# Where the modulation sums of a two-block network stand: three feed-forward stages or two

## The reference, cut to what matters

```
sc, scc = silu(c), silu(c_ctx)
for layer in range(2):
    mod_l = (sc  @ ada_w[layer] + ada_b[layer]).reshape(-1, 9, 1024)
    mod_c = (scc @ ada_w[layer] + ada_b[layer]).reshape(9, 1024)
    x = half_ffn(x, mod[0], mod[1], mod[2], ...)      # x + 0.5*gate*swiglu(rmsnorm(x)*(1+scale)+shift)
    x = x + mod[5] * mixer(rmsnorm(x)*(1+mod[4]) + mod[3])
    x = half_ffn(x, mod[6], mod[7], mod[8], ...)
```

## Time and profile before

| | us |
|---|---|
| median of three runs (lowest, highest) | 2487.13 (2485.32, 2487.84) |
| the profiled execution | 2486.22 |
| its span | 2484.4 |
| TensorE busy | 2417.2 |
| VectorE busy | 1796.4 |
| stage 1, `up0`/`down0` | about 50 to 396 |
| stage 2, `up1`/`down1` | about 609 to 974 |
| stage 3, `up2`/`down2` | about 976 to 1340 |

### The profile page before, as it was taken

How to read it: one execution, slowest core, us unless ns; L and a number is a source line. 1 busy time by engine, 2 the same in 40 slices (tenths; PEclk the granted TensorE clock), 3 DMA queues, 4 the chain that set the end, 5 groups by cost and what they waited for, 6 DMA issues and landing times.

```text
span 2484.4 us, 36330 instructions
## 1 busy us (share of the span) xinstructions
PE 2417.2 (97%) x13814; PEld 2072.6 (83%) x13814; DVE 1796.4 (72%) x2889; ACT 598.9 (24%) x1163; POOL 5.0 (0%) x12
## 2 busy tenths in 40 slices
PE   7999999999999999999999999999998999999998
PEld 5888888767888888888888688888898999898887
DVE  5888887345777667886666568887787776788876
ACT  4000001162111001101002434412265513325401
POOL 0000000000000000000000000000000000000000
PEclk9999999999999999999999999999999999999999
DMA  7555555201444443555553226564543312455563
GB/s 277 173 165 177 173 175 199 90 1 51 152 146 141 143 149 97 183 166 175 168 180 122 90 68 187 187 195 152 157 128 94 103 60 87 135 169 186 183 196 109
DMA packets 98478, 359.65 MB, mean 145 GB/s; under 512 B 10880, under 2 KB 12160, under 8 KB 96832
## 3 DMA queue, kind: packets, MB, share of 16 engines
q1 hardware_dynamic: 96480, 350.37, 45.0%
q0 software_dynamic: 848, 6.77, 0.7%
q10 hardware_dynamic: 1040, 1.05, 0.1%
HBM read 357.10 MB, written 1.05 MB: 144 GB/s over the span
## 4 chain that ended last, share of the span: by engine, by line
PE 93%; DVE 4%; ACT 1%; issue 1%; DMA 0%; SPq 0%; DVEq 0%; ACTq 0%
PE lin L2119 20%; PE lin L2121 19%; PE lin L2120 19%; PE lin L2131 9%; PE lin L2132 5%; PE pair L2322 2%; PE lin L2349 1%; PE lin L2135 1%; PE lin L2205 1%; PE lin L2201 1%; PE lin L2202 1%; PE pair L2736 1%; PE pair L2723 1%; PE lin L2141 1%; PE lin L2143 1%
## 5 line engine op out<-in xcount | busy, mean ns | idle before, releaser
L2119 PE MATMUL lin<-h_all,whi 128*128 128x512 f32 (+1 forms) x1904 | 666.0, 350 | 11.1 <-DVE wlo L1501 5.9
L1501 DVE TENSOR_TENSOR wlo<-raw_all,whi 128x1024 fp32r<-128x1024 f32 (+1 forms) x525 | 631.0, 1202 | 43.0 <-ACT whi L1261 16.4
L2120 PE MATMUL lin<-h_all,whi 128*128 128x512 f32 (+1 forms) x1904 | 658.5, 346 | 0.0
L2121 PE MATMUL lin<-h_all,wlo 128*128 128x512 f32 (+1 forms) x1904 | 658.4, 346 | 0.0
L2119 PEld LDWEIGHTS lin<-h_all,whi 128*128 128x128 f32 x1904 | 361.6, 190 | 60.9 <-issue 9.2
L2120 PEld LDWEIGHTS lin<-h_all,whi 128*128 128x128 f32 x1904 | 361.8, 190 | 43.6
L2121 PEld LDWEIGHTS lin<-h_all,wlo 128*128 128x128 f32 x1904 | 361.4, 190 | 43.7
L1500 DVE CAST whi<-raw_all 128x1024 fp32r<-128x1024 f32 (+2 forms) x396 | 267.0, 674 | 152.0 <-PE lin L2121 109.0
L1890 DVE CUSTOM_DVE_ANT_0 std_all<-raw_all,cond_rows 128x1024 f32<-128x1024 f32 x224 | 273.5, 1221 | 3.3
L2119 PE MATMUL lin<-a_all,whi 128*128 128x512 f32 (+1 forms) x716 | 261.5, 365 | 4.2 <-DVE a_all L935 2.0
L2120 PE MATMUL lin<-a_all,whi 128*128 128x512 f32 (+1 forms) x716 | 260.2, 363 | 0.0
(11 more groups left out here) (374 smaller groups left out, 3030.4 us busy)
## 6 DMA issues: line engine op xcount, KB each, us to landing
raw_all<-w_up SPq DMA_DIRECT2D x176, 512.0 KB, 4.2
raw_all<-w_mod SPq DMA_DIRECT2D x128, 512.0 KB, 3.7
raw_all<-w_down SPq DMA_DIRECT2D x64, 512.0 KB, 4.0
raw_all<-w_exp_up SPq DMA_DIRECT2D x64, 512.0 KB, 3.8
raw_all<-w_exp_down SPq DMA_DIRECT2D x32, 512.0 KB, 4.2
raw_all<-w_down SPq DMA_DIRECT2D x32, 384.0 KB, 3.6
raw_all<-w_b_qk SPq DMA_DIRECT2D x24, 512.0 KB, 3.7
raw_all<-w_b_conv SPq DMA_DIRECT2D x24, 512.0 KB, 3.6
```

What stands on the lines that cost most here:

```text
L1501: dve.tensor_tensor(wlo[s][:, 0:n], r[:, 0:n], whi[s][:, 0:n].bitcast(F32), ALU.subtract)\
L2119: pe.matmul(out_, a, hi[n], start=start and n == 0, stop=False)
L2120: pe.matmul(out_, a, lo[n], start=False, stop=False)
L2121: ins = pe.matmul(out_, b, hi[n], start=False, stop=stop and n == len(cols) - 1)
```

## The change

The stages with tiles are now two, with 64 tiles each; stage 3 has none. So in stages 1 and 2 nearly every step from 4 to 66 has one tile (step 4 has two). Stage 3 loads its weights into all four slots, and its `up` part is a loop on VectorE and SyncE.

```diff
-REGIONS = (("up0", "down0"), ("up1", "down1"), ("up2", "down2"))
-REGION_GROUPS = ((1, 2, 3), (4, 5), (6, 7, 8))
+REGIONS = (("up0", "down0"), ("up1", "down1"))
+REGION_GROUPS = ((1, 2, 3, 4), (5, 6, 7, 8))
...
-                if ph in ("ffn0", "ffn1", "ffn2"):
+                if ph in ("ffn0", "ffn1"):
                     load_region(sp, int(ph[3]))
                     continue
```

## The result

| | median of the runs, us (lowest, highest) | profiled execution | its span |
|---|---|---|---|
| before | 2487.74 (2485.32, 2489.33), five runs beside those of after | 2486.22 | 2484.4 |
| after | 2500.17 (2498.20, 2501.65) | 2501.01 | 2498.8 |

The ratio is 1.0051, with a 95% interval of 1.0037 to 1.0065: 12.4 us slower. Forecast were 8.4 us, 2495.5 in a range up to 2499.0. So the sign was right and the time fell outside the range.

What follows compares the result with a forecast made beforehand. TensorE, busy 2417.2 of 2484.4 us, was taken as the bound. 4.87 + 1.27 + 1.4 + 0.9 = 8.4 us on the profiled 2486.22 gave 2494.7, as a median 2495.5 us; range 2490.3 to 2499.

Steps and rivals of the forecast that it cites:

- Inside stages 1 to 3: Within the three stages, moved sums cost or gain 0 us: TensorE fills the windows and VectorE's work still fits.
- The list of 14.83 us: VectorE's work for three `down0` steps: 14.31 us plus 0.52 for bias additions, fitting under TensorE's 14.96 us.
- The end of stage 1: `ab_uqk` 0 held behind the last tile load; VectorE stands 5.0 us, the last addition before the norm is 4.87 us late.
- The end of stage 2: Same queue order with one-vector tiles: `up2`'s first unit is late, the last addition before the norm 1.27 us late.
- The landing time: At the stage ends, a load behind a tile load lands 4.6 us after issue, as measured; the skill page's estimate was 4.0.
- the first term: Lateness of the last addition at the end of stage 1: 4.87 us, or 4.3 by the skill page's landing.
- TensorE's clock in these norms: Norms after stages 1 and 2: standstill lowers the clock, costing 1.4 us (2.3 if L2173 stays slow) and 0.9 us.
- A: Stage ends: late load mostly covered, landing in 3.7 us; 2491.4 us, or 2487.1 if the queue holds nothing; chance 0.12.
- B: Inside stage 1: VectorE becomes the bound, at 0.2 us over per pair adding 4.4 us, 2500 us; chance 0.06.
- C: Stage 3: matmuls speed up when 64 sums leave, a pair in 10.5 us instead of 10.88, 2482 us; chance 0.03.
- The 0.83 for slower: Whole kernel: chance 0.83 of slower by over 0.2%, against 0.14 within 0.2% and 0.03 faster.

Runs made afterwards that it cites:

- the emptied stage 3: The kernel before without stage 3's 48 tiles, that stage in four slots and loops, stages 1 and 2 keeping 48 and 32 tiles: 2487.67 us, ratio 1.0.
- the second profile: The changed kernel run a second time, unaltered, for another profile: one execution of 2497.90 us.
- The runs with one end mended: Changed kernel, next stage's first two units queued between the last three tile loads of one stage: stage 1 only 2490.53 us, stage 2 only 2497.13 us.
- the hold alone: The kernel before, with SyncE made to wait for the tile of step 64 ahead of `ab_uqk` 0, nothing issued in that wait: 2489.03 us, ratio 1.0006.
- the tiles that end at step 64: The changed kernel with tiles spread over steps 4 to 64 instead of 4 to 66: 2487.43 us, ratio 1.0005.
- the run with more sums: Changed kernel, next stage's first two units queued between the last tile loads at both ends, plus 32 more sums in stage 1: 2512.92 us, ratio 1.0108.
- the version with more busy matmuls: Changed kernel, first units moved forward at both ends, `keep_busy` at 5, 4 and 8 or 6 instead of 3, 3 and 6 or 4: 2486.84 us.

## Why the prediction was wrong

Right, by its own steps:

- *Inside stages 1 to 3, 0.* No wait of TensorE in `up0`; in stage 2 the distance between the two traces is 11.78 us at the start and 11.73 at step 64 of the end; stage 3 to the digit, and the emptied stage 3 at 1.0. The list of 14.83 us for three steps of `down0` was 14.87.
- *The end of stage 1, 4.87 us.* 4.97 and 4.93 in two profiles; wait 5.0 forecast, 5.06 measured; unit issued 3.69 us after the addition, forecast 3.60.
- *The end of stage 2, 1.27 us.* 1.38, and in the second profile 983.64 - 967.20 - 14.96 = 1.48.
- *The landing time.* The Trainium skill, "DMA: Bandwidth & Descriptors", section "Anatomy of one DMA", would have made the load land 4.0 us after its issue, by estimate, and the first term 4.3. Its figures stand there for transfers that GpSimd issues, and these are SyncE's; the measured 4.6 repeated itself.

The step that failed is **TensorE's clock in these norms**, 1.4 + 0.9 = 2.3 us. It was mis-sized: in the means the clock cost 6.5 us (12.9 less 6.35). In the two norms alone it was 2.69 + 1.14 = 3.83 us in the first profile and 3.15 + 0.08 = 3.23 in the second; the rest stood in falls elsewhere, which the sum had at nothing. So it failed in two places.

First, the norm after stage 1. I let the clock come back by L2173, since the fall in the trace of before had lasted 3.4 us. But that fall had no standstill ahead of it. This one lasted 10.2 us (13.6 in the second profile) and covered nearly the whole norm: 2.69 and 3.15 us, beyond even my upper end of 2.3. From the two timelines, start to start: the two L2153 and two L2187 take 2.47 us more, L2173 gives back only 0.11, and the first L2153 starts 0.14 after the addition where it had started 0.20 ahead of it, 0.34. Where I had 2.3 less 0.86 for L2173, it was 2.5 less 0.1, and 0.34 on top. For the second norm I had the pause growing from about 0.5 us; before, TensorE stood still for nothing ahead of it (its last matmul starts at 974.21, L2153 at 974.44), and now for 1.55 and 1.66 us.

Second, I counted only the two norms. The runs with one end mended have 10.2 and 4.6 us more at the lower level, of which the norms explain 6.8 and 3.4 in the profiles. What is left, 3.4 and 1.2 us, is no more than twice what the means are uncertain by; in after it is 6 us (16.2 less 10.2). It stands in falls elsewhere, in the profiles above all in the mixer's pauses. The trace of before had none there. I took it for typical; it was a lucky one: the same two pauses carry a fall in the profiles of the hold alone, of the emptied stage 3 and of the tiles that end at step 64, three kernels whose median is within 2.1 us of before's. Why the falls elsewhere should last longer in the mean behind a late load stays open: single profiles can't count them, and no run told it apart.

The rivals: *A* would have needed a landing of 3.7 us behind a tile load; it was 4.6 us. Its mechanism did appear in the hold alone, where no load stood ahead. *B*, VectorE as the bound, did not decide here, but is one more sum in two tiles away (26 us). *C* had nothing: stage 3's matmuls do not feel VectorE. The 0.83 for slower came out; the range was too narrow upward, because its only unknown cost there was bounded by two norms instead of by what the clock does in a whole run.

## What to carry to other kernels

When work is spread more densely up to the end of a stage, read the in-order load queue across the boundary: a load that waits for a late buffer holds the next stage's first unit behind it, and the cure is the order of three lines in the queue, or a list that ends two steps earlier. Price a new standstill of TensorE by its length and by the clock after it, and take the clock's part from the timed runs (mean clock against time) rather than from one trace, whose falls are partly luck. Here that part was as large as the lateness itself.

## What the hardware showed that I had not expected

- The falls of the clock in these profiles lasted 3.4 us in most cases (behind pauses of 2.4 and 1.8 us in the mixer), 6.8 us in others (at 1672 of before, where the pauses are 0.7 us and less), 10.2 and 13.6 us around the standstill of 5.1 us, and 20.5 us with one of 12 us in the run with more sums.
- With TensorE at the same pauses, the clock falls in one execution and not in the next (2.36 us of idle: L2536 2.69 or 1.97 us).
- In the profile of before the clock is at its lower level for 50.8 us, in that of the version with more busy matmuls for 26.9, and this execution was 4.8 us shorter (2481.41, the fastest of its 11, against 2486.22). Over the runs the difference is 12 us and not 24, and 0.9 us of time. A profile can flatter a version.
- The first of two loads of 512 KB issued 0.4 us apart landed in 3.8 us, the second in 4.6; without one ahead, in the hold alone, one landed in 3.2.
